# Paged latent attention: half of the page columns turned by VectorE, scores in sixteen 32 x 32 tiles, four gathers for each page load

## The reference, cut to what matters

```python
past = cache_l[page_table].reshape(Bd, -1, KV_CACHE_DIM)     # 8 x 4096 x 288
pc, pr = past[..., :256], past[..., 256:]
s_past = einsum('bthc,bkc->bhtk', q_lat, pc) + einsum('bthr,bkr->bhtk', q_rope, pr)
p = softmax(concat([s_past, s_new]) * MLA_SCALE)
ctx = einsum('bhtk,bkc->bthc', p[..., :n_past], pc) + einsum('bhtk,bkc->bthc', p[..., n_past:], nc)
```

## Time and profile before

| what | value |
|---|---|
| median of 3 runs | 1027.32 us (1026.18 to 1028.25) |
| the profiled execution's own time | 1024.94 us |
| its span, first to last instruction | 1023.1 us |
| TensorE busy | 990.5 us, 97% |
| VectorE, ScalarE, GpSimd busy | 521.5, 298.0, 445.7 us |
| granted TensorE clock, mean | 0.992 |
| DMA, mean | 127 GB/s |

### The profile page before, as it was taken

One profiled execution on the slowest core, in us unless ns is written; L12 is line 12 of the kernel. 1 busy time (PEld: TensorE's weight loads), 2 busy tenths in 40 slices (PEclk: granted clock), 3 DMA queues, 4 the chain that ended last, 5 costly groups with the idle time before them and its releaser, 6 DMA issues.

```text
span 1023.1 us, 19800 instructions
## 1 busy us (share of the span) xinstructions
PE 990.5 (97%) x8501; PEld 896.3 (88%) x8501; DVE 521.5 (51%) x732; ACT 298.0 (29%) x598; POOL 445.7 (44%) x284
## 2 busy tenths in 40 slices
PE   6999998998999999999999999999999999999997
PEld 6989898765677777999965899999999999999997
DVE  5889999478555555562255265431342144114413
ACT  7433275465444442220134122210120022002222
POOL 4545687500011102655220255555555555555551
PEclk8999999999999999999999999999999999999998
DMA  8323365504377763622291022322233222322222
GB/s 232 81 68 81 104 198 142 181 20 185 126 278 279 277 269 126 225 84 85 101 401 51 22 83 83 100 87 83 83 89 97 84 83 85 101 84 83 83 83 88
DMA packets 140557, 130.39 MB, mean 127 GB/s; under 512 B 13477, under 2 KB 133170, under 8 KB 136630
## 3 DMA queue, kind: packets, MB, share of 16 engines
q1 hardware_dynamic: 134888, 88.55, 28.7%
q0 software_dynamic: 2304, 37.75, 9.5%
q10 hardware_dynamic: 3278, 2.83, 0.8%
HBM read 123.53 MB, written 5.03 MB: 126 GB/s over the span
## 4 chain that ended last, share of the span: by engine, by line
PE 82%; DVE 12%; ACT 2%; issue 2%; POOL 2%; DMA 1%; SPq 0%; ACTq 0%; DVEq 0%; POOLq 0%
PE gps L582 56%; PE gps L942 5%; PE aux L956 3%; PE aux L983 3%; PE gps L1098 1%; PE gps L1180 1%; PE aux L962 1%; PE gps L1018 1%; DVE act_lo L1689 1%; PE gps L718 1%; PE aux L894 1%; DVE sm L1967 1%; PE aux L1111 1%; PE aux L1132 1%; PE aux L973 1%
## 5 line engine op out<-in xcount | busy, mean ns | idle before, releaser
L582 PE MATMUL gps<-act_hi,whi 128*128 128x272 f32 x912 | 266.5, 292 | 5.2 <-POOL wlo L511 3.4
L497 POOL TENSOR_SCALAR whi<-wraw 128x1024 fp32r<-128x1024 f32 (+1 forms) x109 | 114.5, 1050 | 360.1 <-PE gps L582 299.6
L582 PE MATMUL gps<-act_lo,whi 128*128 128x272 f32 x912 | 265.0, 291 | 0.0
L582 PE MATMUL gps<-act_hi,wlo 128*128 128x272 f32 x912 | 264.5, 290 | 0.0
L500 POOL TENSOR_TENSOR wlo<-wraw,whi 128x1024 fp32r<-128x1024 f32 (+1 forms) x109 | 257.9, 2367 | 9.1
L582 PE MATMUL gps<-h_hi,whi 128*128 128x272 f32 x640 | 186.0, 291 | 0.0
L582 PE MATMUL gps<-h_lo,whi 128*128 128x272 f32 x640 | 185.3, 290 | 0.0
L582 PE MATMUL gps<-h_hi,wlo 128*128 128x272 f32 x640 | 184.8, 289 | 0.0
L582 PEld LDWEIGHTS gps<-act_hi,whi 128*128 128x128 f32 x912 | 173.1, 190 | 6.1 <-issue 3.7
L582 PEld LDWEIGHTS gps<-act_hi,wlo 128*128 128x128 f32 x912 | 173.1, 190 | 0.3 <-issue 0.2
L582 PEld LDWEIGHTS gps<-act_lo,whi 128*128 128x128 f32 x912 | 172.8, 190 | 0.0
(11 more groups left out here) (372 smaller groups left out, 1530.0 us busy)
## 6 DMA issues: line engine op xcount, KB each, us to landing
wraw<-in_w_up_dram SPq DMA_DIRECT2D x32, 512.0 KB, 4.0
wraw<-in_w_down_dram SPq DMA_DIRECT2D x32, 512.0 KB, 3.7
wraw<-in_w_in_dram SPq DMA_DIRECT2D x14, 512.0 KB, 4.2
kv<-in_cache_mem_k_dram SPq DMA_DIRECT2D x7, 1024.0 KB, 6.9
kv<-in_cache_mem_v_dram SPq DMA_DIRECT2D x7, 1024.0 KB, 13.9
wraw<-in_w_mem_k_dram SPq DMA_DIRECT2D x16, 256.0 KB, 3.0
wraw<-in_w_mem_v_dram SPq DMA_DIRECT2D x16, 256.0 KB, 3.2
wraw<-in_w_out_dram SPq DMA_DIRECT2D x8, 512.0 KB, 5.5
```

Source lines behind the costliest of these rows:

```text
L497: nc.gpsimd.tensor_scalar(whi[:, slot, 0:n], wraw[:, slot, 0:n], 1.0, 1.0, ALU.mult, ALU.mult).then_inc(pool_step, 1)
L582: mm = nc.tensor.matmul(out_of(a), w_of(w, k), x_of(x, k, part), start=(k == 0 and s == 0), stop=(k == k_tiles - 1 and s == 2))
```

## The change

- Each half sequence is fetched by four gathers instead of one; each gives every partition four cache rows (4.6 KB). `idx` gets four index columns, made by five small VectorE operations instead of one.
- TensorE turns only latent columns 0 to 127 (16 transposes, `turn(n, part)` in two parts, into two banks of `aux`), and ScalarE alone copies them to `cT`. Columns 128 to 255 are turned by VectorE straight from the page buffer in 32 x 32 blocks, with four block transposes into `cB`, as the rope part already was.
- `score(n)` becomes 80 matmuls of 32 rows x 32 columns x 128 moving columns (sixteen tiles: strip g of the rows, strip j of the columns; strip g writes bank g of `gps`; five rounds x, four of the latent and one of the rope), then 16 matmuls of 128 columns over latent columns 0 to 127. Maximum and exponential read the first 128 columns of the four banks. There is one set of score banks instead of two.
- The queries for this are prepared in the prompt's attention loop: four copies `spread(r)` into `qlr`, eight more transposes (`block_back`), six `by_head` copies instead of two, and four copies `qrope4`, which go behind n = 32. The copies into `qropez` and its memset fall away. `absorb_back`'s result is taken two rounds earlier, `new_rows` goes from n = 28 to n = 30, `gather(2)` waits for `ql_ps` 4 instead of 2.
- TensorE's order becomes `turn(n+1, 0)`, `values(n-1)`, `turn(n+1, 1)`, `turn_p(n)`, `score(n+1)`; the last `values(14)` follows the loop. ScalarE copies two banks ahead of `keep_ctx` and two behind it.

```diff
-        rows_of_pages = cache_mla[0].rearrange("a (e k) n -> (a e) (k n)", e=8)
+        rows_of_pages = cache_mla[0].rearrange("a (e k) n -> (a e) (k n)", e=32)
...
             def gather(n):
-                nc.gpsimd.indirect_dma_start(
-                    pg[n % 4][:, :, :].rearrange("p k d -> p (k d)"), None, rows_of_pages,
-                    bass.IndirectOffsetOnAxis(ap=idx[:, n:n + 1], axis=0)).then_inc(page_in[n % 4], 16)
+                for i in range(4):
+                    nc.gpsimd.indirect_dma_start(
+                        pg[n % 4][:, 4 * i:4 * i + 4, :].rearrange("p k d -> p (k d)"), None, rows_of_pages,
+                        bass.IndirectOffsetOnAxis(ap=idx[:, i, n:n + 1], axis=0)).then_inc(page_in[n % 4], 16)
...
-                    pool.wait_ge(ql_ps, 2)
+                    pool.wait_ge(ql_ps, 4)
                     gather(2)
...
+            def block_back(p):
+                pe.wait_ge(ql_ok, 2 + p)
+                for x in range(2):
+                    for g in range(2):
+                        o = 256 * x + 128 * g
+                        mm = nc.tensor.transpose(W_BANK[:, o:o + 128],
+                                                 qlr[:, g, 2 * p + x, :, :].rearrange("p r d -> p (r d)"), ident[:, :])
+                mm.then_inc(ql_ps, 1)
...
+            def turn(n, part):
+                if part == 0:
+                    pe.wait_ge(page_in[n % 4], 64 * (n // 4) + 64)
+                for i in (2 * part, 2 * part + 1):
+                    k = 4 * n + i
+                    if k >= 2:
+                        pe.wait_ge(g_ta, k - 1)
                     else:
+                        pe.wait_ge(at_exp, 4 * H)
                     for z in range(4):
+                        mm = nc.tensor.transpose(aux[:, 1 + k % 2, 128 * z:128 * z + 128],
+                                                 pg[n % 4][:, 4 * i + z, 0:128], ident[:, :])
                     mm.then_inc(g_T, 1)
...
+                pe.wait_ge(g_rope, n + 1)
+                pe.wait_ge(g_td, 4 * n + 4)
+                for x in range(5):
+                    for g in range(4):
+                        rows = slice(32 * g, 32 * g + 32)
+                        for j in range(4):
+                            q_x, k_x = ((qB[rows, b, x, :], cB[rows, 4 * j:4 * j + 4, 32 * x:32 * x + 32]) if x < 4
+                                        else (qrope4[rows, b, :], ropT[rows, 4 * j:4 * j + 4, :]))
+                            nc.tensor.matmul(gps[32 * j:32 * j + 32, g, 0:128], q_x, k_x, start=(x == 0), stop=False,
+                                             skip_group_check=True)
+                pe.wait_ge(g_ta, 4 * n + 4)
                 for g in range(4):
                     for j in range(4):
                         mm = nc.tensor.matmul(
+                            gps[32 * j:32 * j + 32, g, 0:128], qlat[:, 0, b, :],
+                            cT[:, 512 * j:512 * j + 512].rearrange("p (i g k) -> p g i k", i=4, g=4)[:, g, :, :],
+                            start=False, stop=True, skip_group_check=True)
                 mm.then_inc(g_S, 1)
...
             for n in range(NH - 1):
-                turn(n + 1)
+                turn(n + 1, 0)
+                if n:
+                    values(n - 1)
+                turn(n + 1, 1)
                 turn_p(n)
                 score(n + 1)
-                values(n)
+            values(NH - 2)
             turn_p(NH - 1)
...
             def turned(n):
-                for k in range(8 * n + 1, 8 * n + 8, 2):
-                    dve.wait_ge(g_T, k + 1)
-                    i = k % 8
-                    V.tensor_copy(cT[:, i // 4, 512 * (i % 4):512 * (i % 4) + 512], gps[:, (k + 1) % 4, :]).then_inc(g_td, 1)
+                for j in range(0, 16, 4):
+                    V.transpose(cB[:, j:j + 4, :], pg[n % 4][:, j:j + 4, 128:256]).then_inc(g_td, 1)
```

More of the change, by code:

```diff
@@ L211, in build @@
         qlat = at("qlat", [128, 2, BD, 32], F32, M0 + 43968)
-        qropez = at("qropez", [128, BD, 128], F32, M0 + 46016)
+        qB = at("qB", [128, BD, 4, 32], F32, M0 + 46016)
+        qrope4 = at("qrope4", [128, BD, 32], F32, M0 + 39936)
         ps = [at("ps0", [128, 512], F32, M0 + 50112), at("ps1", [128, 512], F32, R0)]
@@ L948, in score @@
                 b = n // 2
[L949 to L958, removed]
-                pe.wait_ge(g_rope, n + 1)
+                if n == 0:
+                    pe.wait_ge(at_pT, 4 * H)
+                    pe.wait_ge(new_act, 2)
+                    pe.wait_ge(at_lo, 4)
+                pe.wait_ge(g_rope, n + 1)
+                pe.wait_ge(g_td, 4 * n + 4)
[8 more added lines that the diff above has]
+                pe.wait_ge(g_ta, 4 * n + 4)
                 for g in range(4):
@@ L987, in values @@
                 mm.then_inc(g_V, 1)
-            turn(0)
+            turn(0, 0)
+            turn(0, 1)
             for g in range(2):
@@ L1551, in _, with turned @@
                                              scale=1.0, accum_out=sn[:, 1, g:g + 1]).then_inc(new_act, 1)
-            def turned(n):
-                for k in range(8 * n, 8 * n + 8, 2):
+            def turned(n, part):
+                for k in (4 * n + 2 * part, 4 * n + 2 * part + 1):
                     act.wait_ge(g_T, k + 1)
-                    i = k % 8
-                    nc.scalar.copy(cT[:, i // 4, 512 * (i % 4):512 * (i % 4) + 512], gps[:, (k + 1) % 4, :]).then_inc(g_ta, 1)
+                    nc.scalar.copy(cT[:, 512 * (k % 4):512 * (k % 4) + 512], aux[:, 1 + k % 2, :]).then_inc(g_ta, 1)
             def keep_ctx(n):
@@ L1561, in keep_ctx @@
                 nc.scalar.copy(ctxh[:, n, :], aux[:, 3, 0:256]).then_inc(g_cb, 1)
-            turned(0)
+            turned(0, 0)
+            turned(0, 1)
             act.wait_ge(row_out[0], 48)
@@ L1833, in _ @@
             dve.wait_ge(const_in, 16 * 22)
-            V.tensor_scalar(idx[:, :], ptw[:, :], 8.0, lane[:, 0:1], ALU.mult, ALU.add).then_inc(idx_ok, 1)
+            step(V.tensor_scalar(idx[:, 4, :], ptw[:, :], 8.0, lane[:, 0:1], ALU.mult, ALU.add))
+            for i in range(4):
+                ins = V.tensor_scalar(idx[:, i, :], idx[:, 4, :], 4.0, float(i), ALU.mult, ALU.add)
+            ins.then_inc(idx_ok, 1)
             scan(0)
@@ L1915, in _, with spread, by_head @@
                 V.tensor_copy(Kb[R, s, :], kr[R, 0:TP]).then_inc(k_rope, 1)
+            def spread(r):
+                src = gps[:, 2, :].rearrange("p (g c) -> p g c", g=2)[:, :, 128:256]
+                return V.tensor_copy(qlr[:, :, :, r, :], src.rearrange("p g (x d) -> p g x d", x=4))
+            def by_head(dst, x):
+                return V.tensor_copy(dst.rearrange("p b (h t) -> p h b t", t=TD),
+                                     gps[:, 2, x * 256:x * 256 + 256].rearrange("p (h b t) -> p h b t", h=H, t=TD))
             def absorbed(n):
@@ L1937, in absorbed @@
                                        q[R, :, TP:T].rearrange("p h (b t) -> p h b t", t=TD)))
[L1938 removed]
+                elif n == 27:
                     step(V.tensor_reduce(pick[:, :], ident[:, :].rearrange("p (j q) -> p q j", j=4), AX, ALU.add))
[L1940 to L1948 removed]
+                elif n == 31:
                     dve.wait_ge(new_pe, 1)
@@ L1951, in absorbed @@
                     V.tensor_scalar(nmn[:, :], sn[:, 0, :], -1.0, None, ALU.mult).then_inc(new_dve, 1)
+                elif n in (33, 34):
+                    for r in (64 * (n - 33), 64 * (n - 33) + 32):
+                        V.tensor_copy(qrope4[r:r + 32, :, :].rearrange("p b (h t) -> p h b t", t=TD),
+                                      q[R, :, TP:T].rearrange("p h (b t) -> p h b t", t=TD))
             def turned_uk(g):
```

86 lines of the change are left out of this document (39 added, 47 removed).

## The result

The kernel got slower: 1062.88 us (median of 4 runs, 1059.31 to 1064.01) against 1026.99 us for the kernel before on the same chip, a ratio of 1.0338 (95% interval 1.0315 to 1.0361). The forecast was 1005 us.

What follows compares the result with a forecast made beforehand. TensorE, with work in flight for 97% of the span, was taken as the bound. 1024.9 - 26.2 (loop) + 2.3 (queries) + 1.7 (output weights) = 1002.7 us profiled; the median was put at 1005 us, range 998 to 1021.

Steps and rivals of the forecast that it cites:

- The sixteen tiles: Score's 80 small matmuls: all sixteen tiles stream together, 10 rounds of 0.109 us plus about 0.1, 1.19 us; upper end 4.36.
- The loop: Paged loop: half sequences of 6.72 us against 8.53; first interval gains 0.9 us, fourteen more gain 25.3, together -26.2.
- S+4.43: TensorE can begin the sixteen-tile part 4.43 us after S, the end of a score's stream.
- S+4.55: VectorE finishes five transposes of 0.70 us each 4.55 us after a score's stream ends, setting the small tiles' start.
- Queries and the prompt's attention: Prompt's attention: added copies on a full VectorE, less those dropped, cost net +2.3 us; bounds 0 and 4.5.
- The gathers: Four gathers per half sequence: GpSimd issue, landing times and DMA share leave 1.5 us to spare, so they cost nothing.
- The first output weights: Loaded after values(13), their split tile comes late and TensorE waits 1.7 us; bounds 0 and 3.
- Row strips take turns: Rival: in the sixteen-tile part row strips alternate, 4.36 us instead of 1.19, 1054 us in all; chance 0.12.
- turning point of 2.7: Length in us of the sixteen-tile part from which row strips taking turns would decide the outcome.
- Two strips at a time: Rival: only two row strips overlap in the sixteen-tile part, 2.28 us, 1021 us in all; chance 0.08.
- The gathers bound: Rival: smaller pieces make DMA engines need 7.5 us per half sequence, 1012 to 1021 us, say 1015; chance 0.09.
- A full drain at tile changes: Rival: each of five tile shape changes costs 0.27 us instead of 0.09 to 0.15, +8, 1013 us; chance 0.06.

Runs made afterwards that it cites:

- v1: The kernel before with only the rope columns in sixteen 32x32 tiles, record count unchanged, scores copied out by ScalarE and added by VectorE: 1023.19 us, ratio 0.9955.
- e2: The kernel after with each of the 80 small matmuls moving 64 columns instead of 128, half of those scores left out: 1067.45 us.
- e3: The kernel before with its 16 rope matmuls of 128 columns per half sequence cut into 64 of 32, same columns streamed: 1053.42 us.
- e11: The kernel before with its 16 rope matmuls of 128 columns per half sequence cut into 32 of 64, same columns streamed: 1025.80 us.
- e5: The kernel after without gathers beyond the fourth half sequence; later half sequences read the first four pages again: 1049.85 us.
- e4: The kernel after with three of the five rounds of small matmuls, latent columns 192 to 255 left out of the scores: 1026.73 us.
- e7: The kernel after with the row strip loop outside, each strip's tiles taking all five rounds before the next strip's: 1129.09 us.
- e6: The kernel before with each page fetched by four gathers of 4.6 KB pieces, nothing else changed: 1034.64 us, ratio 1.0069.
- e1: The kernel after with one gather of 18.4 KB pieces for each half sequence again: 1077.78 us, ratio 1.0497.
- e9: The kernel after with each page fetched by two gathers of 9.2 KB pieces: 1078.44 us.

## Why the prediction was wrong

**The step that failed** is "The sixteen tiles": 1.19 us for a part that takes, counted to the end of its stream as the sum counts it, 2.16 us at best and 2.72 beside four gathers (2.25 and 2.81 to the next matmul, less the change of 0.09). Half of its reasoning was right: sixteen tiles do run at once. The first 32 records start within 0.24 us in the kernel after, and the 32 of v1 within 0.25. But the part was priced as 10 rounds of streaming with nothing between them; e2 shows that streams are only half of a later round, 0.22 of 0.43 us. Ends taken from rows with at most four tiles at work could not show that. The Trainium skill, "TensorE: Matmul & The Clock Gate", Part 3, gives 10.6 times for sixteen tiles of 512 columns. With 160 passes at 0.109 us (17.4 us one after another) the measured 2.16 us are 8.1 times and 2.72 us are 6.4 times; only v1's single round, some 0.36 us for 3.5, comes near with 9.7. No run here has tiles of 512 columns. For tiles of 128 columns the measurement decides: the gain is smaller, and it depends on what else runs.

**A term was missing:** the supply of instructions. The sum counted what each matmul streams and never how many there are. The change takes a half sequence from 116 to 244 matmul records in less time. e3 (gaps with records added alone), e11 (none with fewer added), v1 (none with sixteen tiles and no records added) and e5 (still there without gathers) speak for this one cause, and the packets' starts 2.2 to 2.9 us ahead of each gap's end show it at work: 21.1 us. **The clock** was the second missing term, some 18 us by the account above. The gaps alone don't settle when it falls: in the kernel after those at 288.94, 360.44 and 371.05 us have no half clock behind them, and in e3 six of eight have none. What brings it down stays open.

**The loop,** forecast at -26.2 us, came to +34.1, 60.3 us away: 20.6 for a half sequence of 8.2 us and not 6.72 (the small part's price), 21.1 for the gaps, 18.6 for half clock and the first interval. With the right price of the small part alone it would have been -5.6, a small gain. So the mis-sized part took the gain, and the two missing terms made the loss.

**What was right.** TensorE ready at S+4.43, VectorE at S+4.55: in e5 the small tiles start at S+4.51. Each block transpose takes 0.61 us and not 0.70, so VectorE is ready 0.4 us earlier than forecast and TensorE's own stream sets the start.

**Queries and the prompt's attention,** +2.3: VectorE starts the rope transpose of the first page at 262.33 us, 63.98 after the first gather; in the kernel before it is 261.97, 64.10 after it. Runs of the same program differ by more than that (63.8 to 64.5 in the kernel after, e2, e4, e5 and e7), so this term is nothing that can be seen, the lower end of its bounds. The +3.1 at the first score's end come from elsewhere:

```profile
265.55 2.59 PE L976 MATMUL gps<-cB,qB 32*32 32x128 f32 x124 [1.87 <-DVE cB L2033]
```

TensorE waits 1.87 us for VectorE, its clock falls at 266.0, and small part and latent matmuls take 5.3 us where 2.17 stood.

**The gathers,** "at nothing": wrong in kind. They cost the kernel before 0.69% (e6), the kernel after 0.57 us in each small part, and yet one gather makes it slower still (e1). The step looked at landing times and DMA share; those were harmless, as said: nothing in the kernel after waits for a page. **The first output weights,** +1.7: no wait in the kernel after, because the loop was slow; 0.94 us in e4, whose 7.06 us come nearest to the 6.72 of the forecast. Right in kind, nearly twice too large.

**The rivals.** "Row strips take turns" gave 1054 us, nearest to the time measured, and is refuted: the part takes 2.16 us without gathers and not 4.36, and v1's takes 0.36 for what in turns is 0.87. It only happens that 2.72 us lies at its turning point of 2.7. "Two strips at a time" has nearly the right size, 2.28 us for the 2.16 without gathers, but not the mechanism: v1's 32 records would need four rounds of 0.109, 0.44 us, and need 0.36, and in the kernel after the first pass of all sixteen tiles starts within 0.10 us. "The gathers bound" is refuted for the kernel after by e5 (the gaps stay without them); in e4, at 7.06 us, there is one wait of 0.6 us for a page. A full drain at tile changes, at this rival's price of 0.27 us, is refuted: the half sequence without a gap has room for 0.1 us each, no more.

## What to carry over

Before cutting a stream into more and smaller matmuls, count the records as well as the columns: here 17 a microsecond over a half sequence did no harm (e11), 24 and more left TensorE without instructions. A smaller tile paid where its part was a single round and the count of records stayed (v1), not where it was five rounds and more than doubled the records. And a price holds in its regime: rows of four tiles at once say little of sixteen, whose later rounds took twice as long as their streams.

## What the runs showed of the hardware

TensorE's instructions come through DMA queue q8 in 16 KB packets, 256 instructions each (3072 more instructions, 12 more packets in e3; 1024 and 4 in e11), and an empty supply shows as "issue" with no releaser. The gaps go with what else is on the DMA engines: the longest was 5.2 us with pieces of 18.4 KB, 3.8 with 9.2 KB, 2.9 with 4.6 KB, and without gathers 1.7 but for one of 4.1 just behind the loads of output weights (e1, e9, the kernel after, e5). Records may start 6.7 ns apart and hold 8.5 ns in column tiles of 32 columns, but 12.8 ns over five rounds of sixteen tiles, where a round takes 0.434 us with 128 columns and 0.327 with 64. Fetching a page in four gathers can hold back TensorE's signals by 0.8 to 1.8 us while its stream goes on.
